# Nine ring rows instead of ten, a fourth weight strip buffer in the freed place, and SBUF buffers moved to multiples of 512 bytes

## What is computed

```python
def block(xb):                                   # 128 tokens
    q = (xb @ w_q).reshape(T, PEER_HEADS, 2, PEER_DHALF)
    s1 = jnp.einsum('thd,hnd->thn', q[:, :, 0], sub_k1)
    s2 = jnp.einsum('thd,hnd->thn', q[:, :, 1], sub_k2)
    ...                                          # top 16 of each half, then of their 256 sums
    eid = e1 * PEER_NKEYS + e2                   # (128 tokens, 8 heads, 16)
    gate = jax.nn.softmax(sc, axis=-1)
    act = jax.nn.gelu(jnp.einsum('td,thkd->thk', xb, u_tab[eid]))
    return jnp.einsum('thk,thkd->td', gate * act, v_tab[eid])

for layer in range(2):
    x = layer_norm(ALPHA * x + mixer(x), ...)
    x = layer_norm(ALPHA * x + peer_ffn(x), ...)
```

## Time and profile before

| | |
|---|---|
| median of three runs | 1807.06 us |
| profiled execution, its own time | 1806.65 us |
| its span, first to last instruction | 1804.5 us |
| TensorE busy | 1544.5 us, 86% of the span |
| VectorE busy | 1063.3 us, 59% |
| ScalarE busy | 604.9 us, 34% |
| GpSimd busy | 579.8 us, 32% |
| moved by DMA | 638.32 MB, mean 354 GB/s |

### The profile page before, as it was taken

The page is one execution under the profiler, slowest core; times in us unless marked ns, Lnnn a source line. Parts: engine busy times, 40 slices in busy tenths (PEclk is TensorE's granted clock), DMA queues, the critical chain, the costliest instruction groups (busy, mean ns, idle before and its releaser), DMA issues.

```text
span 1804.5 us, 18617 instructions
## 1 busy us (share of the span) xinstructions
PE 1544.5 (86%) x6020; PEld 925.0 (51%) x6020; DVE 1063.3 (59%) x2499; ACT 604.9 (34%) x1759; POOL 579.8 (32%) x561
## 2 busy tenths in 40 slices
PE   8999998898777778998899978998999968777776
PEld 7779887754222225763456525763457523222222
DVE  1583543577888865334555447665555568864444
ACT  1434311233333333227532323336632333332222
POOL 2000000334443442333433432334432434444331
PEclk9999858999999999999999999998999999999999
DMA  6222003899999999999999999999999999999996
GB/s 246 95 92 72 1 11 130 342 390 419 419 420 419 420 420 413 419 419 420 419 415 419 414 420 416 420 419 420 419 378 419 405 420 421 419 420 420 420 419 260
DMA packets 92063, 638.32 MB, mean 354 GB/s; under 512 B 11072, under 2 KB 13120, under 8 KB 15424
## 3 DMA queue, kind: packets, MB, share of 16 engines
q0 software_dynamic: 73728, 536.90, 72.0%
q1 hardware_dynamic: 18240, 100.24, 14.3%
HBM read 636.05 MB, written 1.05 MB: 353 GB/s over the span
## 4 chain that ended last, share of the span: by engine, by line
PE 49%; DMA 37%; DVE 6%; ACT 5%; issue 2%; POOL 1%; ACTq 0%; SPq 0%; POOLq 0%; DVEq 0%
DMA arena<-l_peer_uv,arena 34%; PE psum L906 21%; PE psum L588 14%; PE psum L887 4%; DVE arena L1716 3%; DMA wring<-l_w_in 2%; PE psum L765 1%; DMA wring<-l_peer_wq 1%; PE psum L681 1%; PE psum L810 1%; PE psum L671 1%; PE psum L680 1%; ACT L1203 1%; POOL arena L555 1%; ACT early L1216 1%
## 5 line engine op out<-in xcount | busy, mean ns | idle before, releaser
L555 POOL DMA_INDIRECT arena<-l_peer_uv,arena x512 | 566.7, 1107 | 1112.0 <-PE psum L906 851.4
L1716 DVE CUSTOM_DVE_ANT_0 arena<-arena,xres 128x1024 f32<-128x1024 f32 x512 | 620.1, 1223 | 437.8 <-DMA arena<-l_peer_uv,arena 436.4
L906 PE MATMUL psum<-arena,early 128*128 128x512 f32 x1024 | 477.8, 611 | 105.8 <-ACT early L1216 105.8
L906 PE MATMUL psum<-arena 128*128 128x512 f32 x1024 | 476.4, 610 | 106.9 <-ACT arena L1216 106.8
L906 PEld LDWEIGHTS psum<-arena 128*128 128x128 f32 x1024 | 189.8, 193 | 367.9 <-issue 205.6
L906 PEld LDWEIGHTS psum<-arena,early 128*128 128x128 f32 x1024 | 189.4, 193 | 365.4 <-issue 194.6
L588 PE MATMUL psum<-xT,wring 128*128 128x128 f32 (+2 forms) x1856 | 296.5, 320 | 13.6 <-DMA wring<-l_w_in 8.4
L588 PEld LDWEIGHTS psum<-xT,wring 128*128 128x128 f32 (+1 forms) x1856 | 269.2, 192 | 52.5 <-issue 21.0
L1203 ACT ACTIVATE arena<-arena 128x2 f32<-128x2 f32 x256 | 52.1, 203 | 628.4 <-DVE arena L1716 628.2
L1031 ACT COPY arena<-psum 128x256 f32<-128x256 f32 (+2 forms) x138 | 62.5, 471 | 222.6 <-PE psum L588 125.8
L1208 ACT ACTIVATE arena<-arena 128x1 f32<-128x1 f32 x512 | 123.3, 287 | 23.8
(11 more groups left out here) (236 smaller groups left out, 1149.5 us busy)
## 6 DMA issues: line engine op xcount, KB each, us to landing
wring<-l_w_in SPq DMA_DIRECT2D x47, 1024.0 KB, 9.4
wring<-l_peer_wq SPq DMA_DIRECT2D x24, 1024.0 KB, 9.3
wring<-l_w_out SPq DMA_DIRECT2D x12, 1024.0 KB, 11.3
arena<-l_peer_uv,arena POOLq DMA_INDIRECT x512, 17.8
ln_par<-l_ln_g SPq DMA_DIRECT2D x6, 512.0 KB, 12.4
ln_par<-l_ln_b SPq DMA_DIRECT2D x6, 512.0 KB, 15.6
arena<-l_peer_keys SPq DMA_DIRECT2D x2, 1024.0 KB, 7.0
xT<-x_t SPq DMA_DIRECT2D x1, 1024.0 KB, 5.0
```

The costliest lines, as they stand in the source:

```text
L555: pool.indirect_dma_start(out=ring[:, g % RING, :], out_offset=None, in_=T[f"l{l}_peer_uv"], in_offset=bass.IndirectOffsetOnAxis(ap=eid[:, ...
L906: last = mm(self.ps[c], diag[k % DIAGS], ring[:, g % RING, D + c * 512:D + (c + 1) * 512], start=not self.begun, stop=True, skip_group_che ...
L1716: v.tensor_tensor_reduce(out=u, in0=u, in1=xres[:, self.b, :], scale=1.0, scalar=0.0, op0=ALU.mult, op1=ALU.add, accum_out=hid[:, self.b, ...
```

## The change

- `RING` goes from 10 to 9. Everything in `behind(...)` moves down by 8 KB, which frees the last 8 KB of the arena.
- This place is `spare_strip`. From strip 20 on (the first of `peer_q`) the strips go round four buffers, `wring` 0 to 2 and the spare one; until then round three. A load waits for the last strip before it that had the same buffer (`strip_before`); the first load into the spare place waits for the last output bank of layer 0's mixer.
- In the queue of loads one strip more stands ahead of the second load of the keys.
- `sb` makes the small buffers first, then `wring` and `arena`, then the rest. By the sizes `wring`, `arena`, `xres`, `xT` and `ln_par` now all begin at a multiple of 512 bytes.

No arithmetic and no byte of traffic is added or left out.

```diff
-RING = 10
+RING = 9
...
+        iota16 = sb("iota16", [P, TOPK])
+        one_mu = sb("one_mu", [P, RWKV_COLS // P])
+        kn8 = sb("kn8", [P, 8])
+        cexp = sb("cexp", [P, 6])
+        lnst = sb("lnst", [P, NB, 12])
+        lnmv = sb("lnmv", [P, NB, 2])
+        lnrs = sb("lnrs", [P, NB])
+        dcol = sb("dcol", [P, 8])
+        wring = sb("wring", [P, WRING, KT, STRIP])
+        ARENA = 36352
+        A = sb("arena", [P, ARENA])
         ident = sb("ident", [P, P])
...
-        lnst = sb("lnst", [P, NB, 12])
-        lnmv = sb("lnmv", [P, NB, 2])
-        lnrs = sb("lnrs", [P, NB])
-        wring = sb("wring", [P, WRING, KT, STRIP])
-        ARENA = 36352
-        A = sb("arena", [P, ARENA])
-
...
         strip_at = [0]
+        spare_from = next(i for i, s in enumerate(strips) if s[2] == "peer_q")
+        spare_strip = cut(ARENA - KT * STRIP, KT * STRIP).rearrange("p (k n) -> p k n", k=KT)
+        strip_place, strip_load = [], []
+        for i in range(len(strips)):
+            place = i % WRING if i < spare_from else (i - spare_from) % (WRING + 1)
+            strip_place.append(place)
+            strip_load.append(sum(p == place for p in strip_place))
+        strip_before = [max((j for j in range(i) if strip_place[j] == p), default=None)
+                        for i, p in enumerate(strip_place)]
+
+        def strip_buffer(i):
+            return wring[:, strip_place[i]] if strip_place[i] < WRING else spare_strip
...
-            pe.wait_ge(S(f"strip_loaded{n % WRING}"), 16 * (n // WRING + 1))
-            return wring[:, n % WRING]
+            pe.wait_ge(S(f"strip_loaded{strip_place[n]}"), 16 * strip_load[n])
+            return strip_buffer(n)
...
-                    if i >= WRING:
-                        await_filled(sp, strips[i - WRING][2], strips[i - WRING][3])
-                    sp.dma_start(wring[:, i % WRING, :, 0:w], src).then_inc(S(f"strip_loaded{i % WRING}"), 16)
+                    if strip_before[i] is not None:
+                        await_filled(sp, strips[strip_before[i]][2], strips[strip_before[i]][3])
+                    elif strip_place[i] == WRING:
+                        await_filled(sp, "mix_out", 3)
+                    sp.dma_start(strip_buffer(i)[:, :, 0:w], src).then_inc(S(f"strip_loaded{strip_place[i]}"), 16)
...
-            load_strips(WRING)
+            load_strips(WRING + 1)
             await_filled(sp, "peer_s", EH)
             load_keys(1)
             for b in range(NB):
-                load_strips(17 - WRING * (b == 0))
+                load_strips(17 - (WRING + 1) * (b == 0))
```

More of the change, by code:

```diff
@@ L281, in build @@
         causal_ts = sb("causal_ts", [P, SEQ + P])
-        iota16 = sb("iota16", [P, TOPK])
         pars = sb("pars", [P, P])
-        one_mu = sb("one_mu", [P, RWKV_COLS // P])
-        kn8 = sb("kn8", [P, 8])
         small = pars[:, NROWS:NROWS + 4]
-        cexp = sb("cexp", [P, 6])
         def par(name, i=0):
@@ L371, in build @@
         stat = sb("stat", [P, 4, 16])
-        dcol = sb("dcol", [P, 8])
         ring = cut(0, RING * 2 * D).rearrange("p (j n) -> p j n", j=RING)
```

## The result

The changed kernel is faster by 1.1%. Its median over four executions is 1784.59 us (1782.34 to 1791.15), against 1805.94 us of the kernel before in the same series; the ratio is 0.9886, with a 95% interval from 0.9855 to 0.9918. The forecast was 1815 us, with a range from 1790 to 1824: wrong in sign and outside the range. The profiled execution of the changed kernel is the slowest of the four, 1791.15 us with a span of 1789.2 us.

The account below looks back on a forecast made before the run. From 330 us on, bytes through a DMA pipe at 420 GB/s plus pauses. Longer pauses 11.0 us, minus 1.0 at the start, minus about 1 for late strips: 9 us on 1806.65, said as 1815 us; range 1790 to 1824.

Parts of the forecast that it names:

- the one on the addresses: All big buffers move to multiples of 512 bytes; claimed to change no transfer rate, taken as 0.
- The rival: Destinations off a multiple of 512 bytes cost transfer time, so gathers in the row streams speed up; 1796 us, chance 0.17.
- One row less in flight: Row streams from 440 to 690 and from 1436 us: nine ring places still keep 420 GB/s, cost 0.
- One strip more parked: Four unneeded strips lie loaded while rows are awaited, lengthening five later pauses by up to 2.50 us each.
- the places at 710, 924, 1320 and 1416 us: Four of five pauses expected to grow: 2.5 us each at 710, 1320 and 1416, 1.75 at 924.
- The sum of 9 us: Whole kernel: 11.0 us of longer pauses, minus 1.0 at the start, minus about 1 for late strips.
- The pauses: DMA pauses at 710, 924, 1108, 1320 and 1416 us, expected to lengthen by 11.0 us together.
- the start: Between 300 and 330 us one strip more loads ahead of the first gathers; gain between 0 and 2.5, taken as 1.0.
- The pause at 1108 us: At the end of a group of rows the gather queue runs dry; expected to grow by 1.75 us.
- The pause at 376 us: Expected not to grow, since both kernels are full with 13 MB there and TensorE decides.
- Faster waits for strips: TensorE's waits for layer 1 and query strips: the fourth buffer could win at most 0.8 us, taken as 0.

Follow-up runs that it names:

- aligned_only: Kernel before with 32 unused bytes ahead of wring, putting strips and ring at multiples of 512, ten rows and three strip buffers kept; 1783.26 us, ratio 0.988.
- off64: Kernel before with 96 unused bytes ahead of wring, so wring and arena begin 64 bytes behind a multiple of 512; 1801.17 us, ratio 0.9973.
- stream_480: Kernel before, old offset of 480 bytes, with 40 extra plain 1 MB strip loads at its start, eight in flight; 1910.50 us, single execution.
- off256: Kernel before with a pad that puts wring and arena 256 bytes behind a multiple of 512; 1782.22 us, ratio 0.9868.
- ring_aligned: Kernel before with 32 unused bytes behind wring: ring at a multiple of 512, strip buffers still at 480; 1781.64 us, ratio 0.9871.
- ring9_only: Kernel before with nine rows instead of ten, no fourth strip buffer, old offsets; 1808.60 us, ratio 1.0021.
- after_again: The changed kernel itself, run again beside ring10_new_order on the same chip; 1786.46 us, ratio 0.9905 against the kernel before.
- ring10_new_order: Changed kernel with ten rows and three strip buffers again, new addresses kept; 1777.87 us, ratio 0.9868 against the kernel before.
- strips_only: Changed kernel (nine rows, four strip buffers) with buffers in the old order, ring and strips at 480 bytes again; 1807.69 us, ratio 1.002 against the kernel before.
- after_off32: Changed kernel with 32 unused bytes ahead of wring, moving wring, arena and all behind to 32 bytes off; 1807.79 us, ratio 1.0023 against the kernel before.

## Why the prediction was wrong

**The step that failed is the one on the addresses.** "I take 0" was worth 22 us: by aligned_only 1805.09 - 1783.26 = 21.8 us, 1.2%. It rested on one comparison, `xT` at 320 against strips at 480 bytes. Two things were wrong with it. Neither offset is a multiple of 256 (they are 64 and 224 behind one), so both rows show the bad case (off64 and the kernel before differ by 1 GB/s only); the comparison had no good case in it. And both rows lie in the first 9 us of the kernel, where stream_480 shows that even the bad case goes at full rate. The same two windows in the changed kernel, where `xT` and strips lie at 0:

```profile
3.00:4.50 1.50, 0.00 (x0) 0.00 (x0) 0.00 (x0) 0.00 (x0) 1.46 (x4) 1.00 1.01 421
6.00:9.00 3.00, 0.64 (x2) 0.58 (x3) 0.00 (x0) 0.00 (x0) 2.93 (x16) 1.00 0.98 412
```

`xT` has the same 421 GB/s at its new offset, and the strips 412 instead of 426: what set these two rows apart was not the offset. The prediction then let them outweigh a rule that named the border at 256 bytes, and gave the case 0.17.

**The rival had the mechanism right and its size too small.** It took 426 GB/s, the highest rate in any row, as the most there was to win, 8 to 20 us, and 1796 us as its time. The stream rose to 427, which gives 1456 us x (1 - 420 / 427) = 23.9 us if the DMA engines' rate counts for the whole time from 330 to 1786 us. 21.8 were measured in aligned_only, 23.8 in off256 and 23.3 in ring_aligned by the ratios, so all or nearly all of it counted. The lower figure, 8 us, came from counting only stretches in which rows are waited for; the higher, 20, missed little. 1796 us lay in the middle of the two and had the 9 us for the pauses in half of it. That the lead won in the stretches where TensorE is 95% busy is spent at the next wait follows from the total; no run takes it apart. Its condition, that it decides from about 423 GB/s on, was met; where exactly it starts to decide was not tried. Its border, a multiple of 512, is too strict: 256 is enough.

**One row less in flight costs the stream nothing**: right, 420 GB/s in ring9_only and 427 in the changed kernel.

**One strip more parked makes pauses longer**: right in kind. In the changed kernel's profile the places at 710, 924, 1320 and 1416 us lose 13.5 us together where they lost 7.3 (another scale of the full rate, 427 for 420, is in this), and after_again against ring10_new_order says the same. The sum of 9 us was too large for the slow stream, for which it was made: 3.6 us in strips_only (1.1 to 6.1). There the two terms were both off. The pauses, taken at 11.0, grew by 6.7 us in the profile of strips_only and by 4.6 in that of after_off32; the start, taken at 1.0, is worth the whole strip, 2.5 us. For the fast stream after_again against ring10_new_order gives 6.7 to 8.6 us, near the sum, but the changed kernel's first series against aligned_only gives 1 us only (ratios 0.9886 and 0.988, each uncertain by 0.2 to 0.3%), so the size is known to a few us and no better. The cause was argued from the parked strip; ring9_only parks no fourth strip and is as slow, so the tenth row is enough to explain the loss of time. That the parked strip lengthens pauses is likely from the profiles (22.6 us of unused pipe against 19.1), and its early load gives about as much back. The pause at 1108 us, which had 1.75 us in the sum, did not grow in the profile of the changed kernel (the slice there reads 426); at 1320 us it grew by a quarter in one profile and hardly in another. The pause at 376 us was not to grow and didn't.

**Faster waits for strips are worth nothing**: right, the 0.8 us are gone (the sum took off about 1 for them all the same), and ring9_only is no slower than strips_only beyond the interval. That the fourth buffer has a use of its own is not shown by any pair here.

## What to carry to other kernels

In a kernel that streams for long from HBM into SBUF, begin the buffers that most of the bytes go to at a multiple of 256 bytes: here 32 unused bytes ahead of two buffers gave 1.2%, more than all rearranging of waits in this change. To judge such a thing from a profile, look at transfers that belong to a long unbroken stream, and make sure that one of those compared is a good case. In a kernel whose time is bytes through a full pipe, ask of a larger buffer for one kind of transfer where its bytes are taken from: total look-ahead was the same here with nine rows and four strips, and the pauses were as long as, or longer than, those of nine rows and three. And before a few us are explained, see whether they lie in the stretch that was changed: here up to 7 us between two executions came from ahead of it.

## What the runs showed of the hardware

- The rate of a lasting stream of 8 KB pieces into SBUF depends on the destination's offset from a multiple of 256 bytes: 427 GB/s at 0, 421 at 64, 128 and 192, 420 at 32 and 224 (that is 480 mod 256).
- The loss sets in only after 10 to 15 us of unbroken stream (stream_480: 428 GB/s up to 15 us, 419 to 421 after; packets of 8,192 bytes 309.0 ns from 8 to 12 us and 314.6 from 14 to 20 us), with plain loads as with gathers, and a pause of the DMA engines takes it away for as long again (the kernel before: 309.1 ns from 392 to 394 us, behind the pause at 376 us, 315.3 from 400 to 420 us).
- In a mixed stream the loss isn't each transfer's own: with the gathers at 0 the strips at 480 bytes took 309.6 ns a packet, against 315.1 with both at 480 and 309.0 with both at 0 (745 to 875 us).
- The engines' own accesses to the ring change nothing in it: 420 against 427 GB/s with and without them.
